# Delta rule of a two-block network: convolutions, gate curves and the gates' softplus chain planned as lanes of their own

## The chip, the cores and the metric

One Trainium2 chip, one NeuronCore. The time is the device time of one execution of the whole program in microseconds (us), median of three executions. Beside it one execution was taken by the hardware profiler; all rows below are from that one.

## What is computed

Two residual blocks on 512 tokens of width 1024, in fp32, one after the other. The change touches one stage, the gated delta rule that opens the second block. Cut to what matters:

```python
qkv = silu(_causal_dwconv(concat([qa, ka, va]), conv_w))        # 4 taps, 3 x 8 heads of 128 channels
q = l2norm(q) * 128**-0.5;  k = l2norm(k)
beta = sigmoid(beta)
g = -exp(a_log) * softplus(alpha + dt_bias);  G = cumsum(g)      # within chunks of 64 tokens
decay = where(incl, exp(G_i - G_j), 0)
L = where(strict, beta * (k k^T) * decay, 0)
sol = triangular_solve(I + L, [beta*v, beta*exp(G)*k])           # per head and chunk
# scan over 8 chunks: U = u - w S; o = q_dec S + p_intra U; S = S*e + k_dec^T U
oa = rmsnorm(o) * silu(za)
y  = sigmoid(ga) * (oa @ w_a_out) + sigmoid(gb) * (ob @ w_b_out) # ob: band attention, the next stage
x  = x + y @ w_o
```

## The kernel before

**An order made on the host.** `order()` writes one list of steps for the whole program before anything runs. Each of the five engine programs (`tensor_program`, `scalar_program`, `vector_program`, `gpsimd_program`, `sync_program`) walks through this list and issues its own part of every step, so every engine executes in the list's order and waits on semaphores where a result is needed. Within a stage the list is made by `weave()`: several generators ("lanes"), each at a time of its own on a planner's clock, and the lane with the earliest time goes next. The costs by which that clock moves are the table `ROUGH` (engine T, V, A or G, fixed us, us for each block). A step with parts on two engines is one entry of the list: its DVE part and its ACT part take their places in both engines' queues at once.

**The stage.** Weights come in units of 1 MB (256 columns) into two buffers. Each unit is split into a high and a low fp32r part (ScalarE L2002, GpSimd L2800), and a tile of 128 x 512 outputs is 24 matmuls of 512 columns (L1750) into one PSUM bank. The product stream (`products`) has two banks (`sbank`), the other lanes six (`fbank`). The stream makes for each head h the tiles q, k and v (`project`), with the band gate's tiles `gb` after chosen ones, then `za`, `ga` and at the end `wa2`.

**A tile's way.** `dq1` multiplies the bank by the row of norms (L2268) into one of two padded buffers, which frees the bank, and starts the convolution with the first tap (L2572). `dq2` is the other three taps in one step (L2578), `dq3` is SiLU on ScalarE (L2128). The three steps stand in the product stream itself, behind the tile's matmuls. `project(h)` begins once head h-2 is prepared to the end, since the convolved q, k, v have two places each. `GATES_AFTER` says where `gb` tiles (`band_gate`, step `gb`: L2268, then Sigmoid L2209) go in.

**The gates.** `gates1` (L2268, Sigmoid L2106), `gates2` (softplus, with Exp L2109 and Ln L2112) and `gates3` (cumulative sum, Exp L2115) follow one another in the lane `gates()` with no yield between them. Their results, turned and split, are what every head's decay needs (`rct`, `rlo`).

**A head.** `prepare(h)` starts once `cooked` holds h (q, k and v all through SiLU), head h-2 is inverted and the pair before the last is scanned. It turns k (`p8`), forms k k^T (`p11`), sums squares (`p2`, L2139), and `p4` makes the decay: two DVE operations, Exp on ScalarE (L2143), five small DVE operations and a multiplication. `p12` multiplies k k^T by it (L2629). Then `invert(h)` (two lanes, even and odd heads) begins with `i1` (L2648, L2650), turns the matrix on TensorE (L1781, copy back L2163) and goes through five levels of two products each (L1786; DVE L2655, L2659). `i7u` and `i7w` apply the inverse; each has its product and its copy (L2169) in one step. `scan(g)` runs over the eight chunks of a pair of heads (L1904, L1913, L1923, L1926; DVE L2673, L2685), `gate(g)` norms and multiplies by silu(za) (step `za`: L2268, Silu L2179), `ga` is L2268 and Sigmoid L2183, `ya` multiplies the projected output by it (L2706), `ysum` and `yop` do so for the other branch and split the sum for `w_o`.

## Time and profile before

| | us |
|---|---|
| median of 3 executions | 2621.57 (2620.88 to 2621.96) |
| profiled execution, its own time | 2616.85 |
| its span, first to last instruction | 2615.6 |
| the changed stage in it | about 1196 to 1747 |
| TensorE busy, share of the span | 2525.3 (97%) |

The profiled execution was 4.7 us (0.18%) shorter than the median. A matmul's busy time overlaps the next one's: a busy TensorE is one that waits for nothing, not one at its peak. The granted clock has two levels, 2.4 GHz (1.00) and 1.2 GHz.

### The profile page before, as it was taken

Reading aid. Unit: us, or ns where it says so; the run is one execution under the profiler, and the core shown is the slowest. Engines: PE = TensorE matmul, PEld = TensorE weight load, DVE = VectorE, ACT = ScalarE, POOL = GpSimd, SP = SyncE. Lnnn points to the kernel's source line nnn. Section 1 sums busy time; section 2 is a strip of 40 time slices with the busy share of each in tenths; the row PEclk is TensorE's granted clock in tenths of the full one; section 3 lists DMA queues with packets and bytes.
Section 4 is the critical chain, followed back from the end, with each engine's and each line's share of the span. In section 5 each row is a group of like instructions: output and inputs, shape, how many; then the busy total and the mean of one; then the engine's idle time right before and its main releaser. Section 6 shows DMA issues by size and latency. Waiting matters only on the chain.

```text
span 2615.6 us, 32476 instructions
## 1 busy us (share of the span) xinstructions
PE 2525.3 (97%) x12760; PEld 2076.0 (79%) x12760; DVE 1054.0 (40%) x2281; ACT 951.9 (36%) x1448; POOL 1171.1 (45%) x1565
## 2 busy tenths in 40 slices
PE   7999999999999999999999999999999999999997
PEld 5777888888777888887888888877767887888886
DVE  6964111125963111125657664413444423310112
ACT  4553322234553222234434333315453434321221
POOL 5115665653115655654323221453224664565653
PEclk9999999999999999999999999999999999999999
DMA  4442223224532223223111110132212322222222
GB/s 160 126 113 81 97 83 103 97 89 141 135 95 81 97 94 108 92 80 119 65 49 49 49 49 33 65 113 81 90 57 97 113 97 81 97 87 99 99 91 76
DMA packets 41367, 237.27 MB, mean 91 GB/s; under 512 B 4736, under 2 KB 5888, under 8 KB 18560
## 3 DMA queue, kind: packets, MB, share of 16 engines
q1 hardware_dynamic: 38912, 218.43, 24.0%
q0 software_dynamic: 2304, 16.78, 3.2%
q8 instruction: 101, 1.65, 0.3%
q14 instruction: 50, 0.41, 0.1%
HBM read 214.22 MB, written 4.19 MB: 84 GB/s over the span
## 4 chain that ended last, share of the span: by engine, by line
PE 84%; DVE 9%; ACT 3%; POOL 2%; issue 1%; DMA 1%; SPq 0%; DVEq 0%; ACTq 0%; POOLq 0%
PE PB L1750 68%; PE PB L1752 3%; PE PB L1786 3%; POOL WL L2800 2%; DVE cc L2409 1%; PE PB L1770 1%; ACT WH L2002 1%; PE PB L1938 1%; PE PB L1762 1%; PE PB L1957 1%; PE PB L1945 1%; PE PB L1822 1%; PE PB L1781 1%; PE PB L1969 1%; PE PB L1985 1%
## 5 line engine op out<-in xcount | busy, mean ns | idle before, releaser
L2800 POOL TENSOR_TENSOR WL<-WR,WH 128x256 fp32r<-128x256 f32 (+1 forms) x1444 | 1043.5, 759 | 876.6 <-ACT WH L2002 876.6
L1750 PE MATMUL PB<-HH,WH 128*128 128x512 f32 x1992 | 805.2, 404 | 14.6 <-ACT HH L2017 9.8
L1750 PE MATMUL PB<-HL,WH 128*128 128x512 f32 x1992 | 782.6, 393 | 2.0 <-DVE HL L2303 2.0
L1750 PE MATMUL PB<-HH,WL 128*128 128x512 f32 x1992 | 519.4, 396 | 1.1 <-POOL WL L2800 1.1
L1750 PEld LDWEIGHTS PB<-HH,WH 128*128 128x128 f32 x1992 | 377.6, 190 | 105.5 <-issue 15.6
L2002 ACT ACTIVATE WH<-WR 128x2048 fp32r<-128x2048 f32 (+1 forms) x209 | 371.5, 1778 | 227.7 <-PE PB L1750 221.4
L1750 PEld LDWEIGHTS PB<-HL,WH 128*128 128x128 f32 x1992 | 377.6, 190 | 80.1 <-issue 4.6
L1750 PEld LDWEIGHTS PB<-HH,WL 128*128 128x128 f32 x1992 | 366.4, 189 | 74.6 <-issue 3.4
L1750 PE MATMUL PB<-BL,WH 128*128 128x512 f32 x848 | 334.1, 394 | 0.8 <-DVE BL L2312 0.8
L1750 PE MATMUL PB<-BH,WH 128*128 128x512 f32 x784 | 311.5, 397 | 2.7 <-ACT BH L2031 2.7
L1750 PE MATMUL PB<-BH,WL 128*128 128x512 f32 x784 | 196.4, 395 | 4.5 <-POOL WL L2800 4.5
L2318 DVE TENSOR_TENSOR X<-X,PB 128x512 f32<-128x512 f32 x80 | 54.9, 687 | 354.6 <-PE PB L1750 354.6
L1750 PEld LDWEIGHTS PB<-BL,WH 128*128 128x128 f32 x848 | 160.8, 190 | 37.2 <-DVE BL L2312 1.5
L1750 PEld LDWEIGHTS PB<-BH,WH 128*128 128x128 f32 x784 | 148.8, 190 | 37.7 <-ACT BH L2031 4.4
L1750 PEld LDWEIGHTS PB<-BH,WL 128*128 128x128 f32 x784 | 147.9, 189 | 38.6 <-POOL WL L2800 5.7
L2813 POOL TENSOR_TENSOR BL<-ff1c,BH 128x512 fp32r<-128x512 f32 x44 | 56.9, 1294 | 169.7 <-ACT BH L2031 169.7
L2031 ACT ACTIVATE BH<-ff1c 128x512 fp32r<-128x512 f32 x44 | 27.8, 632 | 233.3 <-DVE ff1c L2501 233.3
L2268 DVE TENSOR_TENSOR ff1b<-PB,RSTD 128x512 f32<-128x512 f32 x44 | 30.4, 691 | 196.5 <-PE PB L1750 196.5
L2268 DVE TENSOR_TENSOR ff1a<-PB,RSTD 128x512 f32<-128x512 f32 x44 | 30.4, 692 | 174.6 <-PE PB L1750 167.7
L2806 POOL DMA_DIRECT2D WL<-WR x16 | 14.1, 884 | 190.1 <-ACT WL L2005 190.1
L2409 DVE SCALAR_TENSOR_TENSOR cc<-cp,VECS,cc 128x512 f32<-128x512 f32 x120 | 93.3, 830 | 0.0
L2017 ACT ACTIVATE HH<-X,VECS 128x512 fp32r<-128x512 f32 x48 | 33.2, 718 | 122.5 <-DVE X L2318 122.5
(348 smaller groups left out, 2933.0 us busy)
## 6 DMA issues: line engine op xcount, KB each, us to landing
WR<-in_w_gu SPq DMA_DIRECT2D x66, 1024.0 KB, 4.8
WR<-in_w_dn SPq DMA_DIRECT2D x48, 704.0 KB, 4.0
WR<-in_w_in SPq DMA_DIRECT2D x22, 1024.0 KB, 4.9
WL<-WR POOLq DMA_DIRECT2D x16, 1024.0 KB, 7.5
WR<-in_qkv SPq DMA_DIRECT2D x12, 1024.0 KB, 4.9
WR<-in_w_out SPq DMA_DIRECT2D x8, 1024.0 KB, 4.8
WR<-in_qk SPq DMA_DIRECT2D x8, 1024.0 KB, 4.9
WR<-in_gb SPq DMA_DIRECT2D x4, 1024.0 KB, 4.9
```

What stands on the lines that cost most here:

```text
L1750: ins = pe.matmul(out[:, 0:n], wt[:, k * cols + j * P:k * cols + (j + 1) * P], x[:, k, 0:n], start=first, stop=last)
L1752: ins = pe.matmul(out[:, 0:cols], x[:, k, j * P:(j + 1) * P], wt[:, k * cols:(k + 1) * cols], start=first, stop=last)
L1762: ins = pe.matmul(out[:, j0 + b:j0 + b + 1], blk(src, b), ones[:, 0:1], start=(j0 == 0 and b == 0), stop=(b == nb - 1), skip_group_check=True)
L1786: ins = pe.matmul(blk(PB[t.b], i), blk(left, i), blk(right, i), start=True, stop=True)
L2002: a.activation(m.WH[u % 2][:, 0:n], m.WR[u % 2][:, 0:n], ACT.Copy).then_inc(sems["whi"], 1)
L2017: a.activation(m.HH[:, c, :], m.X[:, c, :], ACT.Copy, scale=w["gain"]).then_inc(sems["hh"], 1)
L2031: a.activation(high[:, w["c"], :], w["src"], ACT.Copy).then_inc(sems["bh"], 1)
L2268: v.tensor_tensor(dst, PB[t.b][:, 0:bank_cols], m.RSTD[:], ALU.mult).then_inc(sems[name], 1)
L2318: v.tensor_tensor(m.X[:, c, :], m.X[:, c, :], PB[w["tile"].b][:], ALU.add).then_inc(sems["res"], 1)
L2409: v.scalar_tensor_tensor(m.cc[j][:], m.cp[j][:, k:k + S], vec(f"dw_w{l}", 2 * k + j), m.cc[j][:], ALU.mult, ALU.add).then_inc(sems["tap"], 1)
L2800: ins = g.tensor_tensor(m.WL[u % 2][:, part], m.WR[u % 2][:, part], f32(m.WH[u % 2][:, part]), ALU.subtract)
L2813: g.tensor_tensor(m.BL[:, w["c"], :], w["src"], f32(high[:, w["c"], :]), ALU.subtract).then_inc(sems["blg"], 1)
```

## The change

- The convolution leaves the product stream. `dq1` is now only the multiplication that frees the bank. Each of the four taps is a step `dq2` with a key of its own, in a new lane `convolutions()`, with SiLU (`dq3`) a step behind them. A tap waits for `read[j]` of head h-2 (that the old q, k or v has been read), each of the three alone. The stream no longer waits for head h-2; it waits for a free padded buffer.
- `prepare(h)` starts when the keys are through SiLU (`curved[1]`), and its second half waits for q and v. A new `due()` holds it in the plan until the planner's clock says that the signal is there.
- `gates2` becomes `soft1`, `soft2`, `soft3` with a yield behind each.
- `p4` is split into `p4`, `p4n`, `p4d`; the curves of `za`, `ga` and `gb` become steps `zact`, `gact`, `gbact`, the last two in lanes of their own; `i7u` and `i7w` do their products together and then the copies `i8u`, `i8w`.
- Sigmoid of `ga` and `gb` becomes Tanh of half the argument; `ya` and `ysum` multiply by (t + 1) in the same instruction and `yop` takes the factor 0.5.
- `ROUGH` gets new costs for these steps.

```diff
-    "gates1": [("V", 0.8, 0), ("A", 1.9, 0)], "gates2": [("V", 1.5, 0), ("A", 2.0, 0), ("V", 0.6, 0), ("A", 1.9, 0), ("V", 3.0, 0)],
-    "gates3": [("V", 2.0, 0), ("A", 3.0, 0)], "gates4": [("T", 0.5, 0), ("A", 0.5, 0)], "gates5": [("A", 1.4, 0), ("V", 0.8, 0)],
-    "rs2": [("V", 3.5, 0)], "nt": [("V", 0.9, 0)], "dq1": [("V", 1.3, 0)], "dq2": [("V", 2.5, 0)], "dq3": [("A", 1.3, 0)],
+    "gates1": [("V", 0.7, 0), ("A", 1.9, 0)], "soft1": [("V", 1.2, 0), ("A", 2.1, 0)], "soft2": [("V", 0.5, 0), ("A", 1.9, 0)], "soft3": [("V", 2.6, 0)],
+    "gates3": [("V", 2.4, 0), ("A", 2.6, 0)], "gates4": [("T", 0.5, 0), ("A", 0.5, 0)], "gates5": [("A", 1.4, 0), ("V", 0.8, 0)],
+    "rs2": [("V", 3.5, 0)], "nt": [("V", 0.9, 0)], "dq1": [("V", 0.72, 0)], "dq2": [("V", 0.78, 0)], "dq3": [("A", 1.3, 0)],
...
-"p4": [("V", 1.5, 0), ("A", 0.7, 0), ("V", 1.2, 0)], "p6": [("V", 3.5, 0)], "p5": [("T", 0.5, 0)],
+"p4": [("V", 1.4, 0), ("A", 2.0, 0)], "p4n": [("V", 0.85, 0)], "p4d": [("V", 0.75, 0)], "p6": [("V", 2.4, 0)], "p5": [("T", 0.5, 0)],
...
@@ project
-                pd = pads.take()
-                step("dq1", h, j, tile=t, pad=pd.i, after=pd.after, c_after=cfree["qkv"[j] + str(i)])
+                while all(x.held for x in pads.rooms):
+                    yield
+                pad_of[h, j] = pd = pads.take()
+                step("dq1", h, j, tile=t, pad=pd.i, after=pd.after)
                 room.free(at("dq1", h, j))
                 yield
-                step("dq2", h, j, pad=pd.i)
-                pd.free(at("dq2", h, j))
-                yield
-                step("dq3", h, j)
...
+        def convolutions():
+
+            for h in range(8):
+                for j in range(3):
+                    while (h, j) not in pad_of:
+                        yield
+                    yield from until((read[j], h - 2))
+                    pd = pad_of[h, j]
+                    for k in (3, 2, 1, 0):
+                        step("dq2", h, j, k, pad=pd.i, tok=at("dq1", h, j), c_after=cfree["qkv"[j] + str(h % 2)])
+                        if k == 0:
+                            pd.free(at("dq2", h, j, 0))
+                        yield
+                    step("dq3", h, j)
+                    curved[j].add(h)
+                    yield
+
+        def curves_b():
+            for c in range(DC):
+                while c not in gb_in:
+                    yield
+                step("gbact", c, tok=at("gb1", c))
+                gb_out.add(c)
+                yield
...
@@ prepare
             ready.add(h)
             yield
+            yield from until((curved[0], h), (curved[2], h))
+            yield from due(at("dq3", h, 2))
...
+        def due(*signals):
+
+            while clock.known(list(signals)) > max(clock.lane, clock.free["T"]):
+                yield
...
@@ products
             for h in range(8):
-                yield from until((prepared, h - 2))
                 yield from project(h)
...
@@ preparations
-                yield from until((cooked, h), (inverted, h - 2), (scanned, h // 2 - 2))
-                yield
-                yield
+                yield from until((curved[1], h), (inverted, h - 2), (scanned, h // 2 - 2))
+                yield from due(at("dq3", h, 1))
...
-            a.activation(m.SGA[:, c, :], m.SGA[:, c, :], ACT.Sigmoid).then_inc(sems["ga"], 1)
+            a.activation(m.SGA[:, c, :], m.SGA[:, c, :], ACT.Tanh, scale=0.5).then_inc(sems["ga"], 1)
...
-            v.tensor_tensor(m.SGA[:, c, :], PB[w["tile"].b][:], m.SGA[:, c, :], ALU.mult).then_inc(sems["ya"], 1)
+            v.scalar_tensor_tensor(m.SGA[:, c, :], m.SGA[:, c, :], 1.0, PB[w["tile"].b][:], ALU.add, ALU.mult).then_inc(sems["ya"], 1)
```

## Rows read from the trace of the kernel before

**Rows 1.** The page's first line.

```profile
span 2615.6 us, 32476 instructions
```

**Rows 2.** Windows: from:to, length, busy us and instructions by engine, PEclk, DMA share, GB/s.

```profile
1196.00:1747.00 551.00, 528.75 (x3121) 453.86 (x3120) 316.35 (x723) 209.18 (x365) 173.39 (x233) 0.99 0.17 59
...
1220.00:1240.00 20.00, 19.55 (x89) 16.17 (x90) 16.26 (x25) 10.50 (x19) 8.97 (x11) 0.91 0.15 53
1240.00:1260.00 20.00, 15.98 (x84) 13.55 (x83) 13.11 (x31) 11.54 (x19) 10.27 (x14) 0.91 0.16 53
```

**Rows 3.** Waits of TensorE in 1196 to 1747: waiter, releaser, us, times, longest.

```profile
PE PB L1781 <- DVE ZZ L2650: 7.0, 6, 4.0
PE PB L1786 <- ACT TT L2163: 6.1, 3, 2.1
PE PB L1750 <- DVE pad L2268: 4.9, 2, 3.4
```

**Rows 4.** Timeline of TensorE: start, us, line, operands, count, [idle before it].

```profile
1205.79 0.50 PE L1750 MATMUL PB<-HH,WH 128*128 128x512 f32 x1 [1.41 <-DVE pad L2268]
...
1214.13 0.39 PE L1750 MATMUL PB<-HH,WH 128*128 128x512 f32 x1
1214.36 0.39 PE L1750 MATMUL PB<-HL,WH 128*128 128x512 f32 x1
...
1220.45 0.50 PE L1750 MATMUL PB<-HH,WH 128*128 128x512 f32 x1 [3.44 <-DVE pad L2268]
...
1222.16 0.63 PE L1750 MATMUL PB<-HH,WH 128*128 128x512 f32 x1
1222.58 0.63 PE L1750 MATMUL PB<-HL,WH 128*128 128x512 f32 x1
...
1245.87 1.09 PE L1781 MATMUL PB<-CON,ZZ 128*128 128x128 f32 x4 [4.02 <-DVE ZZ L2650]
...
1347.41 1.54 PE L1786 MATMUL PB<-TT,UM 128*128 128x128 f32 x8 [2.07 <-ACT TT L2163]
...
1521.14 1.26 PE L1786 MATMUL PB<-TT,UM 128*128 128x128 f32 x8 [1.99 <-ACT TT L2163]
```

**Rows 5.** Timeline of DVE: the multiplication that ends the first long wait.

```profile
1219.71 0.69 DVE L2268 TENSOR_TENSOR pad<-PB,RSTD 128x512 f32<-128x512 f32 x1
```

**Rows 6.** Timeline of DVE and ACT before the wait that ends at 1347.41.

```profile
1342.73 3.38 DVE L2578 SCALAR_TENSOR_TENSOR ck<-pad,VECS,ck 128x512 f32<-128x512 f32 x3
...
1346.15 0.63 ACT L2128 ACTIVATE ck<-ck 128x512 f32<-128x512 f32 x1 [5.09 <-DVE ck L2578]
1346.69 0.58 ACT L2163 ACTIVATE TT<-PB 128x512 f32<-128x512 f32 x1
```

**Rows 7.** Timeline of ACT: the first head's exponential, and two later heads'.

```profile
1238.95 1.28 ACT L2209 ACT_TABLE_LOAD   x1
...
1240.90 1.28 ACT L2143 ACT_TABLE_LOAD   x1
1242.19 0.63 ACT L2143 ACTIVATE DT<-DT 128x512 f32<-128x512 f32 x1
...
1473.72 0.63 ACT L2143 ACTIVATE DT<-DT 128x512 f32<-128x512 f32 x1 [2.56 <-DVE DT L2591]
...
1539.47 0.63 ACT L2143 ACTIVATE DT<-DT 128x512 f32<-128x512 f32 x1 [0.36 <-DVE DT L2591]
```

**Rows 8.** Groups by line in 1474 to 1539, TensorE: count, busy us, mean ns.

```profile
L1750 PE MATMUL PB<-HH,WH 128*128 128x512 f32 x38 | 16.8, 441 | 0.0
```

**Rows 9.** Groups by line in 1195 to 1750: count, busy us, mean ns, idle before.

```profile
L2578 DVE SCALAR_TENSOR_TENSOR cq<-pad,VECS,cq 128x512 f32<-128x512 f32 x24 | 18.0, 751 | 0.8
...
L2209 ACT ACT_TABLE_LOAD x5 | 6.4, 1283 | 0.1
...
L2694 DVE SCALAR_TENSOR_TENSOR O<-O,VECS,PB 128x512 f32<-128x512 f32 x8 | 5.9, 743 | 3.5 <-PE PB L1770 3.5
...
L2706 DVE TENSOR_TENSOR SGA<-PB,SGA 128x512 f32<-128x512 f32 x8 | 5.5, 692 | 40.4 <-PE PB L1750 40.4
```

More of the change, by code:

```diff
@@ L1030, in gates @@
             bank0.free(at("ab"))
-            step("gates2", after=f)
+            step("soft1", after=f)
+            yield
+            step("soft2", after=f)
+            yield
+            step("soft3", after=f)
+            yield
             step("gates3", after=f)
@@ L1094, in project, with curves_a @@
                         yield from band_gate()
-            cooked.add(h)
+        pad_of = {}
+        def convolutions():
[16 more added lines that the diff above has]
+                while c not in gb_in:
+                    yield
+                step("gbact", c, tok=at("gb1", c))
+                gb_out.add(c)
+                yield
+        def curves_a():
+            for c in range(DC):
+                while c not in ga_in:
+                    yield
+                step("gact", c, tok=at("ga1", c))
+                ga_out.add(c)
+                yield
         kn_done = [[], []]
@@ L1112, in prepare @@
             step("p4", h, tile=t, after=dt_after[0] + hf)
+            step("p4n", h, tile=t)
+            yield
+            step("p4d", h, tile=t)
             room.free(at("pdn", h))
@@ L1124, in prepare @@
             cfree[f"v{i}"] = [t4.done]
+            read[2].add(h)
             step("p1", h, q=qq.i, after=qq.after)
@@ L1185, in invert @@
             yield from until((prepared, h))
-            yield from fbank.left(1)
-            room = fbank.take()
-            t = Tile(room, room.after)
-            pe("i7u", h, tile=t, after=st_after)
-            room.free(at("iut", h))
-            yield from fbank.left(1)
-            room = fbank.take()
-            t = Tile(room, room.after)
-            ifree[f"Z{i}"] = half_after[i] = [pe("i7w", h, tile=t, after=st_after)]
-            room.free(at("iwt", h))
+            yield from fbank.left(2)
+            room, t = row("i7u", h)
+            room2, t2 = row("i7w", h)
+            ifree[f"Z{i}"] = half_after[i] = [t2.done]
+            step("i8u", h, tile=t, after=st_after)
+            room.free(at("iut", h))
+            step("i8w", h, tile=t2, after=st_after)
+            room2.free(at("iwt", h))
             yield
@@ L1249, in gate @@
                     yield
+                step("zact", h, tok=at("za1", h))
+                yield
                 yield from fbank.left(1)
@@ L1274, in gate_tiles @@
                 drain(itg)
-        cooked, ready, prepared, inverted, scanned, gated, gated_heads = (set() for _ in range(7))
+        ready, prepared, inverted, scanned, gated, gated_heads = (set() for _ in range(6))
+        curved, read = [set() for _ in "qkv"], [set() for _ in "qkv"]
         def until(*conditions):
@@ L1306, in products @@
                     room, t = x
+                    while c not in ga_out:
+                        yield
                     step("ya", c, tile=t)
@@ L1355, in operands @@
                 yield
-        weave(clock, products(), 0.0, lane(gates(), preparations()), inversions(0), inversions(1), scans(), gatings(), last_gating(), operands())
+        weave(clock, products(), 0.0, lane(gates(), preparations()), inversions(0), inversions(1), scans(), gatings(), last_gating(), operands(),
+              convolutions(), curves_b(), curves_a())
     def band_attention(xs):
@@ L2106, in scalar_program @@
             a.activation(m.R[32:64, :], m.UM[0][32:64, :], ACT.Sigmoid).then_inc(sems["beta"], 1)
-        elif kind == "gates2":
+        elif kind == "soft1":
             ae.wait_ge(*at("dtb"))
@@ L2163, in scalar_program @@
             a.activation(m.TT[key[0] % 2][:], PB[w["tile"].b][:], ACT.Copy).then_inc(sems["it"], 1)
-        elif kind in ("i7u", "i7w"):
+        elif kind in ("i8u", "i8w"):
             h, = key
@@ L2528, in vector_program @@
             times_rstd(m.UM[0][:], w["tile"], "ab")
-        elif kind == "gates2":
+        elif kind == "soft1":
             ve.wait_ge(*at("ab"))
@@ L2567, in vector_program @@
             ve.all(w["after"])
[L2568 removed]
             times_rstd(m.pad[w["pad"]][:, 3:3 + S], w["tile"], "dq1")
[L2570 to L2572 removed]
         elif kind == "dq2":
[L2574 to L2581 removed]
+            h, j, k = key
+            c, pad = m.cqkv[h % 2][j], m.pad[w["pad"]]
+            tap = vec("conv2", 24 * k + 8 * j + h)
+            if k == 3:
+                ve.wait_ge(*at("dq1", h, j))
+                ve.all(w["c_after"])
+                v.tensor_scalar(c[:], pad[:, 3:3 + S], tap, None, ALU.mult).then_inc(sems["dq2"], 1)
+            else:
+                ve.wait_ge(*at("dq2", h, j, k + 1))
+                v.scalar_tensor_tensor(c[:], pad[:, k:k + S], tap, c[:], ALU.mult, ALU.add).then_inc(sems["dq2"], 1)
         elif kind == "p4":
```

64 lines of the change are left out of this document (30 added, 34 removed), and 12 rows, old and new, of tables (KINDS, ROUGH).

## The prediction

> **What bounds the kernel now.** I read the page's head first [rows 1], then windows over the changed stage [rows 2], TensorE's list of waits in it [rows 3], its timeline at the longest waits [rows 4], and for each the timelines of the engine named [rows 5 to 7]. In the stage's 551.0 us TensorE is busy for 528.75: it waits 22.25 us, and DVE (316 us), ScalarE (209 us) and GpSimd (173 us) are far from full. So the stage is bound by TensorE's own work, and neither fewer DVE nor fewer ScalarE microseconds are worth anything as such. What an order of steps can give back is the 22.25 us and what follows from it. The clock is the second part: four stretches of 20 us (from 1220, 1240, 1340 and 1520; the first two in [rows 2]) show a granted clock of 0.91 instead of 1.00, each one with a wait of about 2 to 4 us before or in it. Behind the wait that ends at 1220.45 the engine falls to the 1.2 GHz level: matmuls that start 0.23 us apart at 1214 start 0.42 us apart at 1222 [rows 4]. A mean of 0.91 over 20 us is 3.6 us at half speed, which costs at most 1.8 us; I count seven matmuls 0.2 us too long in the first stretch, 1.4 us. I take 1.5 for each of four, 6.0 us in all.
>
> So the ceiling of the change is about 22.25 + 6 = 28 us, 1.1% of the kernel. The rest of this text sorts that sum by cause.
>
> **The gates' chain in one piece.** TensorE waits 3.44 us until 1220.45 for a product bank, and the DVE multiplication that would free it starts only at 1219.71 [rows 4, 5]. A tile is 24 matmuls 0.225 us apart, 5.4 us; the one in question began at 1205.79 [rows 4] and was done by about 1211.4. Its `dq1` stands in DVE's queue behind gates2 and gates3. With a yield behind each of soft1, soft2 and soft3, a `dq1` of 0.69 us can stand between them. Then the wait goes, and the half-speed stretch with it: 3.4 + 1.5 = 4.9. The other 1.5 us of L2268's 4.9 [rows 3] come before, when the norms themselves are made, and the change leaves them. What is late next: the gates' results, by the DVE work that is let in front of them, one or two `dq1` and a few taps, 0.7 to 4 us. Behind them stands the first head's decay.
>
> **The first head.** TensorE waits 4.02 us for the first inversion's matrix [rows 4]. Two things work on it. Before, head 0 waits until q, k and v are all through SiLU, and head 1's q convolution is in DVE's queue ahead of its decay (four taps, of which three take 2.3 us in the mean, [rows 9]); now it starts with k alone. I rebuild DVE's work from 1205 with the durations of the trace: dq1 and taps of q 3.6, ab and soft1 1.9, dq1 of k 0.7, soft2 and soft3 3.3, gates3 2.3, dq1 of v 0.7, taps of k 2.9, splitting the gates 3.1: about 1224. Add the decay (1.4, the exponential with its load 1.9, four more operations 2.8) and some 3 us for what else is let in: the first matrix is there at 1233 to 1237, not at 1245.8. Dense work for TensorE up to there is q, k, v, q of head 1 and two `gb` tiles at 5.4 us each, which reaches to about 1236. The second is ScalarE's side: 1.28 us for a table load for the band gate's Sigmoid at 1238.95, 0.63 us for the curve, and 1.28 us for a load back at 1240.90 lie directly ahead of that exponential [rows 7]. Either is enough for most of the 4.02. I take 4.0 + 1.5 = 5.5. If the dense cover is short by the time the gates' chain gets longer, up to 4 us of it stay.
>
> The Trainium skill bears on the second part (ScalarE: Activation LUTs, *Table sets: the hidden batching unit*): tanh is in the set that has exp as its anchor, so Tanh beside Exp needs one load and not two. By it one of the two 1.28 us loads at 1238.95 and 1240.90 goes, and the others of L2209 that stand behind an exponential. The same page prices a switch at about 2.66 us with its drain, and by that the chain of head 0 would gain 2.66 us instead of 1.28; this case's trace shows the activation 0.01 us behind the 1.28 us load, so the trace disagrees with the drain. None of this enters the sum, which has the 4.02 us once whichever part removes it.
>
> **The convolution in one piece.** Three waits of TensorE, 6.1 us, are for L2163, the copy of a turned matrix [rows 3]. The one that ends at 1347.41 shows why [rows 6]: DVE works on three taps without a break, from 1342.73 for 3.38 us, SiLU on them waits in ScalarE's queue for 5.09 us and runs at 1346.15, and the copy, whose input TensorE made at 1344, comes behind SiLU at 1346.69. The waiting instruction blocks its queue. In the new list SiLU is a step that comes when the plan has the last tap done, and the copy, planned earlier, stands ahead of it. All three have this form (1521.14 is another). The waits go, and with them two of the four half-speed stretches, those of 1340 and 1520: 6.1 + 3.0 = 9.1. What can remain: a tap can now stand between an inversion's own DVE steps, 0.75 us in the mean [rows 9] and up to 1.13 where GpSimd is busy [rows 6]; and with wrong costs SiLU can still be planned too early. I keep 2 us of it: 7.1.
>
> **The decay's cost in the plan.** Five more waits for L2650, together 7.0 - 4.0 = 3.0 us [rows 3], come at the start of a head's inversion: the plan had 0.7 us for an exponential that takes 1.28 + 0.63 = 1.9 [rows 7], so TensorE's turn came about 1.2 us early. The new cost is 2.0. I take 2.0 of the 3.0.
>
> **What costs nothing.** The new instructions are as many as the old ones. `ya` and `ysum` change from a two-input multiplication to one with a scalar, of which the trace has 692 ns (L2706) and 743 ns (L2694) for the same size [rows 9]: 0 to 0.05 us each, 24 of them with `yop`. DVE idles 40.4 us before the eight L2706 [rows 9], so this hides behind the projection's matmuls; without cover it is at most 1.2 us. Tanh is not in the trace; the nearest row is the exponential of the same size, 0.63 us [rows 7], and a table load of 1.28 us more or less. A set for tanh of its own would be loaded where Sigmoid's is now, five times for L2209 [rows 9] and twice for L2183, so no worse than before. Every DMA keeps its order and number; SP's queue only follows the units. The joint products i7u and i7w ask for three free banks of six instead of two, which can hold a lane back, not TensorE.
>
> **The sum.** 4.9 + 5.5 + 7.1 + 2.0 = 19.5 us gone. Against it I set new waits. The old order lost 22.25 us in 551; some 10 of it are taken by these terms' twins in any order: DVE slowed from 0.75 to 1.13 us by GpSimd, copies behind a 1.9 us split on ScalarE, none of it in the plan. A different order meets these at other places. I take 5 us (between 0 and 12). Net: 14.5. Against the profiled execution, 2616.85 - 14.5 = 2602.4; the median of the runs shown lies 4.7 us higher, so 2607.
>
> **The rivals.**
> 1. *All of it comes* and few new waits appear: 19.5 us or more, up to 28: 2602 down to 2594. For it speaks that heads start some 10 us earlier, so that the plan always has something ready. Against: nothing in the plan knows of contention.
> 2. *New waits take the place of the old.* Finer steps give as many chances to be wrong as before; the four causes go and others of 10 to 17 us in total come. Net 8 us to a loss of 4: 2614 to 2626. For it: 2 us of TensorE's waits are enough to lose 1.5 more by the clock.
> 3. *The filler is used up too early* (slower). The stream no longer waits for head h-2, so it can run ahead by two padded buffers and two banks, four tiles. Between the exponentials of head 5 (1473.72) and head 6 (1539.47) [rows 7] TensorE has the last q, k, v tiles and scans as dense and small work: 38 high matmuls are 4.8 tiles [rows 8]. Four of them moved ahead leave 4 x 5.4 = 21.6 us of that gap to be filled by two inversions and a scan alone. If these can't, it costs 21.6 and two half-speed stretches, 3.0, less the 14.5: 2607 + 24.6 = 2632. It decides from 14.5 us lost there. Against it: the small work in the gap fills about 35 us by itself, and the gap shrinks as the chains get TensorE sooner; the work moved ahead is not lost.
> 4. *The table loads decide*: silu, exp and tanh alternate more often, each 1.28 us on ScalarE. ScalarE is busy 209 of 551 us, so ten more loads show only where TensorE waits for a copy. This is part of rival 2.
>
> **How the numbers follow.** The likeliest case, 9 to 19 us gained, 2602 to 2613: 0.50. Rival 1, below 2602: 0.18. Rivals 2 and 4, 2613 to 2626: 0.21. Rival 3, above 2626: 0.11. The predicted time is 2607. For 8 in 10 I go from 2596, where only the ceiling's last two microseconds are left out, to 2622, into rival 2. About 0.2% (5.2 us) is what a measurement of this kernel can tell from no change. Faster than 2616.3: the first two cases and a third of rival 2, 0.75. Within 0.2%: the rest of rival 2, 0.14. Slower: rival 3 whole, 0.11.
>
> **What would show it.** In the profile after: no wait on L2268 of 3 us near 1215 to 1220; the first L1781 on ZZ before 1240 with no 4 us before it; no wait of about 2 us on L2163's copy; in ScalarE's timeline SiLU of a convolution starting within 1 us of getting to the queue's head; granted clock 1.00 in nearly all 20 us stretches; in total 8 to 13 us of TensorE waiting in the stage. The prediction is wrong if TensorE's waits add up to 20 us at other places, if the stage's busy time itself grows (more changes between dense and small matmuls), or if waits gather between head 5 and head 6.

## The result, and the profile after

The changed kernel takes 2586.97 us (median of 4 runs, 2585.19 to 2594.96) where the kernel before, run beside it, takes 2621.23 us (median of 4, 2615.5 to 2621.96). The medians are 34.3 us apart (1.3%); the ratio over all the runs is 0.9886, 95% interval 0.9871 to 0.9900, so 1.0 to 1.3% faster. The forecast was 2607 with a range of 2596 to 2622. The sign was right; the size was outside the range, on the side of rival 1 and beyond it.

The page of the profile after, its first line and the busy time of the engines (device time of this execution 2587.04 us):

```profile
span 2585.7 us, 32474 instructions
...
PE 2513.4 (97%) x12760; PEld 2069.5 (80%) x12760; DVE 1051.3 (41%) x2281; ACT 943.9 (37%) x1440; POOL 1181.1 (46%) x1565
```

The windows over the changed stage, with the same 3,121 to 3,123 matmuls as [rows 2], and the four stretches that had a granted clock of 0.91 before:

```profile
1195.50:1719.50 524.00, 518.85 (x3123) 449.99 (x3122) 314.72 (x723) 201.22 (x357) 182.07 (x233) 1.00 0.18 62
...
1220.00:1240.00 20.00, 20.00 (x98) 16.72 (x97) 15.60 (x26) 13.17 (x23) 9.65 (x13) 1.00 0.31 106
1240.00:1260.00 20.00, 19.06 (x110) 16.20 (x110) 16.80 (x38) 8.01 (x15) 8.85 (x12) 1.00 0.28 96
1340.00:1360.00 20.00, 20.00 (x128) 17.62 (x128) 13.58 (x27) 9.57 (x20) 7.00 (x8) 1.00 0.04 6
1520.00:1540.00 20.00, 20.00 (x132) 17.65 (x131) 15.45 (x39) 8.38 (x18) 6.17 (x8) 1.00 0.15 53
```

TensorE is idle for 5.2 us of 524, where it was 22.25 of 551, and the clock is 1.00 throughout; the prediction had 8 to 13 us of waiting. The list of TensorE's waits in this stage (L1799 is the dense matmul, L1750 before; L1830 the turns, L1781 before; L2318 was L2268, L2714 was L2659):

```profile
PE PB L1799 <- DVE pad L2318: 1.4, 1, 1.4
PE PB L1799 <- POOL WL L2855: 1.3, 1, 1.3
PE PB L1830 <- DVE ZZ L2714: 1.1, 2, 0.9
PE PB L1819 <- DVE STAT L2392: 0.7, 1, 0.7
PE PB L1962 <- DVE UU L2728: 0.6, 1, 0.6
```

All that was named in [rows 3] is gone but for 1.4 of L2268's 4.9. The lines of 1.4, 1.3 and 0.7 stand in the list of before too. New are only 1.1 + 0.6 = 1.7 us.

The gates' chain, DVE's timeline: DVE now waits for TensorE's tiles (last brackets), where TensorE waited for DVE in [rows 4, 5].

```profile
1210.98 0.69 DVE L2318 TENSOR_TENSOR pad<-PB,RSTD 128x512 f32<-128x512 f32 x1 [2.01 <-PE PB L1799]
1211.59 0.74 DVE L2631 SCALAR_TENSOR_TENSOR cq<-pad,VECS,cq 128x512 f32<-128x512 f32 x1
...
1216.49 0.69 DVE L2318 TENSOR_TENSOR pad<-PB,RSTD 128x512 f32<-128x512 f32 x1 [3.82 <-PE PB L1799]
```

The first head, TensorE's timeline: the turn of the first inversion runs at 1247.06 with no wait.

```profile
1245.49 0.60 PE L1830 MATMUL PB<-CON,cv 128*128 128x128 f32 x4
...
1247.06 0.60 PE L1830 MATMUL PB<-CON,ZZ 128*128 128x128 f32 x4
```

But its input is not early. DVE's row that ends it starts at 1243.24:

```profile
1243.24 0.69 DVE L2705 TENSOR_TENSOR ZZ<-CON,ZZ 128x512 f32<-128x512 f32 x1
```

The forecast had the matrix at 1233 to 1237; it was there at 1243.9, 39.5 us after the stage's first padded product, where it took 40.7 us before. TensorE came to the place of this turn 36.8 us after that product before, and 42.6 us after it now, since the plan has a dense tile, a turn and two small groups ahead of it (1240.05 to 1247.06). So the wait went for the larger part by the turn's later place, and for 1.3 us of the 4.0 by an earlier matrix.

ScalarE and the convolutions. These groups (count, busy us, mean ns, then ScalarE's idle time before them and what ended it) are L2128 of the kernel before:

```profile
L2128 ACT ACTIVATE cv<-cv 128x512 f32<-128x512 f32 x8 | 5.1, 632 | 24.2 <-DVE cv L2578 24.2
...
L2128 ACT ACTIVATE cq<-cq 128x512 f32<-128x512 f32 x8 | 5.1, 632 | 23.5 <-DVE cq L2578 23.5
...
L2128 ACT ACTIVATE ck<-ck 128x512 f32<-128x512 f32 x8 | 5.0, 631 | 30.2 <-DVE ck L2578 30.2
```

and the same after, with the table loads left there:

```profile
L2178 ACT ACT_TABLE_LOAD x8 | 10.3, 1283 | 0.1
L2193 ACT ACT_TABLE_LOAD x8 | 10.3, 1283 | 0.1
L2178 ACT ACTIVATE cq<-cq 128x512 f32<-128x512 f32 x8 | 5.0, 629 | 0.1
L2178 ACT ACTIVATE cv<-cv 128x512 f32<-128x512 f32 x8 | 5.0, 628 | 3.7 <-DVE cv L2631 3.7
L2178 ACT ACTIVATE ck<-ck 128x512 f32<-128x512 f32 x8 | 5.0, 627 | 5.3 <-DVE ck L2631 5.2
```

SiLU held ScalarE's queue for 24.2 + 23.5 + 30.2 = 78 us while it waited for taps, and now for 9. That is the mechanism of [rows 6], and the change removes nearly all of it. The loads of the band gates (L2209, five, and L2183, two) are gone.

### The profile page after: what moved, and what is told of

It reads as the page before. It is cut to its first block, busy times and chain, and to the rows that moved or that the text cites. A ratio compares the mean times of both kernels' runs of the same rounds, so it can differ in the third digit from the quotient of the medians.

```text
span 2585.7 us, 32474 instructions
## 1 busy us (share of the span) xinstructions
PE 2513.4 (97%) x12760; PEld 2069.5 (80%) x12760; DVE 1051.3 (41%) x2281; ACT 943.9 (37%) x1440; POOL 1181.1 (46%) x1565
## 3 DMA queue, kind: packets, MB, share of 16 engines
q1 hardware_dynamic: 38912, 218.43, 24.2%
## 4 chain that ended last, share of the span: by engine, by line
PE 88%; DVE 7%; POOL 2%; ACT 1%; issue 1%; DMA 0%; SPq 0%; DVEq 0%; ACTq 0%; POOLq 0%
PE PB L1799 71%; PE PB L1835 4%; PE PB L1801 3%; DVE cc L2459 2%; POOL WL L2855 2%; PE PB L1830 1%; PE PB L1811 1%; PE PB L1819 1%; PE PB L2006 1%; PE PB L1987 1%; PE PB L1994 1%; PE PB L1871 1%; PE PB L2034 1%; PE PB L2018 1%; PE PB L1975 1%
## 5 line engine op out<-in xcount | busy, mean ns | idle before, releaser
L1799 PE MATMUL PB<-HH,WH 128*128 128x512 f32 x1992 | 801.5, 402 | 11.3 <-ACT HH L2066 9.9
L1799 PE MATMUL PB<-HL,WH 128*128 128x512 f32 x1992 | 779.5, 391 | 1.9 <-DVE HL L2353 1.9
L1799 PE MATMUL PB<-HH,WL 128*128 128x512 f32 x1992 | 520.6, 396 | 1.1 <-POOL WL L2855 1.1
L1799 PEld LDWEIGHTS PB<-HH,WH 128*128 128x128 f32 x1992 | 375.9, 189 | 101.9 <-issue 16.0
L1799 PEld LDWEIGHTS PB<-HL,WH 128*128 128x128 f32 x1992 | 375.9, 189 | 80.5 <-issue 4.8
L1799 PEld LDWEIGHTS PB<-HH,WL 128*128 128x128 f32 x1992 | 365.0, 188 | 74.7 <-issue 4.4
L1799 PE MATMUL PB<-BL,WH 128*128 128x512 f32 x848 | 332.8, 392 | 0.8 <-DVE BL L2362 0.8
L1799 PE MATMUL PB<-BH,WH 128*128 128x512 f32 x784 | 309.7, 395 | 2.7 <-ACT BH L2080 2.7
L1799 PE MATMUL PB<-BH,WL 128*128 128x512 f32 x784 | 196.7, 395 | 4.5 <-POOL WL L2855 4.5
L1799 PEld LDWEIGHTS PB<-BL,WH 128*128 128x128 f32 x848 | 159.7, 188 | 36.9 <-DVE BL L2362 1.5
L1799 PEld LDWEIGHTS PB<-BH,WL 128*128 128x128 f32 x784 | 148.1, 189 | 38.7 <-POOL WL L2855 5.7
L1799 PEld LDWEIGHTS PB<-BH,WH 128*128 128x128 f32 x784 | 148.0, 189 | 38.1 <-ACT BH L2080 5.1
L2318 DVE TENSOR_TENSOR ff1b<-PB,RSTD 128x512 f32<-128x512 f32 x44 | 30.4, 691 | 196.5 <-PE PB L1799 196.5
L2318 DVE TENSOR_TENSOR ff1a<-PB,RSTD 128x512 f32<-128x512 f32 x44 | 30.4, 692 | 175.2 <-PE PB L1799 167.7
```

The lines of the kernel that those rows point to most:

```text
L1799: ins = pe.matmul(out[:, 0:n], wt[:, k * cols + j * P:k * cols + (j + 1) * P], x[:, k, 0:n], start=first, stop=last)
L2318: v.tensor_tensor(dst, PB[t.b][:, 0:bank_cols], m.RSTD[:], ALU.mult).then_inc(sems[name], 1)
```

## Where the 30 us of the profiled executions went

I cut the span at two events that every version has: the start of the first padded product (1205.0 before, 1204.5 after) and the start of the last `ya` (1744.0, 1716.3). TensorE issues 3,069 or 3,070 matmuls between them in every version. The windows of exactly these stretches, of the kernel before:

```profile
1205.00:1744.00 539.00, 518.07 (x3069) 445.76 (x3070) 310.80 (x705) 205.40 (x363) 164.39 (x221) 0.99 0.16 55
```

and after:

```profile
1204.50:1716.30 511.80, 508.06 (x3070) 441.75 (x3071) 309.19 (x706) 197.46 (x354) 173.07 (x221) 1.00 0.17 58
```

The stage is 27.2 us shorter. Idle TensorE: 20.9 to 3.7, 17.2 us. The clock: four stretches at 0.91 are 4 x 20 x 0.09 = 7.2 us, and after there is none. The other 2.8 us are busy time that neither explains. Outside the stage the profiled executions differ by another 2.7 us: 0.5 ahead of it, 6.4 in the stretch behind it (275.7 to 269.3), and 4.2 back in the rest. The stretch behind it ends at the last `SGA<-SGA,X` (2019.7 and 1985.6). From the last `ya` to the end of the program both kernels, and all versions below, give TensorE the same instructions in the same order, and the stretch takes 267.8 to 276.9 us in them. In the kernels before (first line) and after TensorE is idle there for the same 16.8 us, and the clock differs:

```profile
1744.00:2019.70 275.70, 258.91 (x1581) 203.74 (x1581) 110.80 (x329) 122.91 (x282) 97.36 (x144) 0.96 0.25 88
1716.30:1985.60 269.30, 252.46 (x1580) 199.01 (x1579) 111.46 (x328) 122.77 (x282) 98.52 (x144) 0.99 0.25 86
```

The kernels with the old steps have 268.6 to 275.7 us there and those with the new ones 267.8 to 276.9, so I don't count the 6.4 as the change's.

All kernels of this study by the same cut. Clock is the sum of 20 us times (1 - granted clock) over the stretches of 20 us in the stage; the medians stand beside a kernel before of 2619.9 to 2621.4 us in each group of runs.

```
                                    stage  busy   idle  clock  median us  ratio, 95%
before                              539.0  518.1  20.9   7.2   2621.23
after                               511.8  508.1   3.7   0.0   2586.97    0.9871 to 0.9900
e1_before_newcosts                  554.1  523.0  31.1  15.8   2631.03    1.0026 to 1.0051
e2_sigmoid                          511.8  508.1   3.7   0.0   2591.70    0.9864 to 0.9918
e4_all_three                        510.7  507.3   3.4   0.0   2586.58    0.9844 to 0.9900
e3_throttle                         520.9  512.5   8.4   5.2   2603.25    0.9920 to 0.9956
e5_gates_one                        519.9  510.8   9.1   1.8   2595.16    0.9883 to 0.9919
e6_taps_one                         522.0  509.3  12.7   0.0   2596.40    0.9893 to 0.9944
e8_old_costs                        519.5  512.0   7.5   3.4   2595.57    0.9886 to 0.9936
e13_three_undone                    536.7  520.0  16.7  15.6   2610.68    0.9953 to 0.9981
e10_stall                           520.9  510.5  10.4   3.4   2602.31    0.9915 to 0.9962
f1_line                             513.9  508.5   5.4   0.0   2590.87    0.9855 to 0.9901
new steps, costs: p1_costs_up  +6%  543.3  523.4  19.9  13.8   2622.32    0.9998 to 1.0020
                  p3_up3       +3%  524.3  512.7  11.6   3.4   2605.47    0.9913 to 0.9959
                  p4_down3     -3%  516.9  511.3   5.6   3.4   2593.52    0.9884 to 0.9926
                  p2_costs_down -6% 510.4  506.8   3.6   0.0   2592.15    0.9868 to 0.9922
old steps, costs: q1_old_up    +6%  546.5  520.4  26.1  10.6   2625.65    1.0014 to 1.0037
                  q3_old_up3   +3%  550.1  522.6  27.5  14.0   2625.41    1.0002 to 1.0025
                  q4_old_down3 -3%  533.9  517.2  16.7   5.4   2610.04    0.9960 to 0.9979
                  q2_old_down  -6%  548.1  525.6  22.5  15.4   2622.68    0.9999 to 1.0025
```

Busy time less clock is 507 to 512 us in all but one (504 in e13). (The idle 3.7 and 20.9 us are less than the 5.2 and 22.25 above: a wait of 0.7 us and the first half of the one of 1.4 us lie ahead of the cut.) So the stage is some 509 us of TensorE's work, plus its idle time, plus the clock. The clock's part tends to grow with the idle part, none at 3.7 us and 7 to 16 where some 20 us or more are idle, but loosely: none at 12.7 us in e6. It is one profiled execution of each kernel, while one kernel's executions differ by up to 10 us (2585.19 to 2594.96 for after); a difference of a few us between two rows needs the medians beside it.

## The experiments

**The costs alone on the old steps** (e1_before_newcosts; the new planner costs of the head's preparation, the gates and the taps in the kernel before):

```
-  "p4": [("V", 1.5, 0), ("A", 0.7, 0), ("V", 1.2, 0)], "p6": [("V", 3.5, 0)]
+  "p4": [("V", 1.4, 0), ("A", 2.0, 0), ("V", 1.6, 0)], "p6": [("V", 2.4, 0)]
...
-  "dq1": [("V", 1.3, 0)], "dq2": [("V", 2.5, 0)]
+  "dq1": [("V", 1.2, 0)], "dq2": [("V", 2.34, 0)]
```

> The kernel before with the planner's new costs alone (gates, p4, p6, dq1, dq2), no step split. Theory A (the finer steps make the gain): the five short waits for the first turn of a head go and the early 4 us wait shrinks, but the waits of about 2 us on the copy L2163 and the 3.4 us wait for the product bank stay: 3 to 8 us faster than before, 2613 to 2618. Theory B (the right costs make the gain): 15 us or more faster, under 2606. Theory C (each order is a draw): anywhere within 10 us of before.

2631.03 us, 10 us slower than before. Theories A and B missed; C, a draw within 10 us of before, is missed by 0.4 us. The waits that the prediction had tied to the costs did go (L2650 has one of 1.8 us left of 7.0), but others grew or came:

```profile
PE PB L1786 <- ACT TT L2163: 8.1, 5, 3.6
PE PB L1750 <- DVE pad L2268: 4.9, 2, 3.4
PE PB L1786 <- DVE YY L2655: 4.5, 2, 3.5
```

Better costs by themselves gave a worse order here.

**One part undone at a time.** The stream of projections limited to two heads ahead again (e3_throttle):

```
             for h in range(8):
+                yield from until((prepared, h - 2))
                 yield from project(h)
```

> The new kernel with one line put back: the product stream waits until head h-2 is prepared to the end. Theory A: the running ahead isn't what helps; within 4 us of the new kernel, 2583 to 2591. Rival: dense tiles ready early are the cover that the old order lacked; waits come back, 2595 or more.

The four taps and SiLU in one piece (e6_taps_one):

```
                             pd.free(at("dq2", h, j, 0))
-                        yield
                     step("dq3", h, j)
```

> The new kernel with the four taps and SiLU of a convolution planned as one piece again (no yield between them), still in a lane of their own. Theory A: the waits of about 2 us on the copy of a turned matrix come back, three or more of them with their half-speed stretches, +6 to +12 us against the new kernel: 2593 to 2599. Theory B: nothing, since the costs are right: 2585 to 2590.

The gates' chain in one piece (e5_gates_one; its third gate tiles also wait for the last value head, a line that f1_line tries alone):

```
             step("soft1", after=f)
-            yield
             step("soft2", after=f)
-            yield
             step("soft3", after=f)
-            yield
```

> The new kernel with soft1, soft2, soft3 and gates3 in one piece (and the gate tiles waiting for the last v besides). Theory A: the wait of 3 to 4 us for a product bank near 1217 comes back and a half-speed stretch behind it: +5 us, 2592. If the new order had room for it anyway: no change within 2 us.

The old costs of a head and of the convolution in the new steps, the gates' costs staying new (e8_old_costs):

```
-  "p4": [("V", 1.4, 0), ("A", 2.0, 0)], "p4n": [("V", 0.85, 0)], "p4d": [("V", 0.75, 0)], "p6": [("V", 2.4, 0)]
+  "p4": [("V", 1.5, 0), ("A", 0.7, 0)], "p4n": [("V", 0.6, 0)], "p4d": [("V", 0.6, 0)], "p6": [("V", 3.5, 0)]
...
```

> The new kernel with the old planner costs for a head (exponential of the decay 0.7 us instead of 2.0, p6 3.5 instead of 2.4, the convolution's 3.15 in all). The first experiment showed the new costs alone in the old steps to be slower by 10 us. Theory A (finer steps make the gain, costs add little): 2587 to 2594. Theory B (both are needed: a plan of fine steps is only as good as its costs): waits for the first turn of each head come back, eight of 0.5 to 2 us with half-speed stretches, 2597 or more.

The stages are 9.1, 10.2, 8.1 and 7.7 us longer than after's, the medians 16.3, 9.4, 8.2 and 8.6. e3 met its rival (2595 or more), e6 the time of its theory A by other waits than that theory's, e5 lost more than its theory A, and e8 fell between its two. For none of them is the loss mainly the return of the wait that the prediction had tied to the part. e3 has 2.9 us at `YY` and 1.7 at `SMALL`. Of the gates' 3.44 us wait e5 has 1.24 back:

```profile
1217.86 0.50 PE L1796 MATMUL PB<-HH,WH 128*128 128x512 f32 x1 [1.24 <-DVE pad L2315]
```

e8's list has no wait for the first matrix of a head. e6 brings SiLU's hold on ScalarE back, here its three groups,

```profile
L2177 ACT ACTIVATE cv<-cv 128x512 f32<-128x512 f32 x8 | 5.1, 632 | 21.8 <-DVE cv L2630 21.8
L2177 ACT ACTIVATE cq<-cq 128x512 f32<-128x512 f32 x8 | 5.1, 632 | 19.5 <-DVE cq L2630 19.5
L2177 ACT ACTIVATE ck<-ck 128x512 f32<-128x512 f32 x8 | 5.1, 632 | 23.3 <-DVE ck L2630 23.3
```

65 us of idle ScalarE against 9, but none of TensorE's 2 us waits for the turned copy: its waits are 4.2 us at `YY` and 2.3 at `ZZ`. A blocked ScalarE costs nothing where the order has nothing of TensorE's behind it.

**The three structural parts undone together** (e13_three_undone, the edits of e3, e5 and e6 in one):

> The new kernel with three parts undone together: the stream waits for head h-2, the taps are one piece, the gates' chain is one piece. Alone they cost the stage 9.1, 10.2 and 8.1 us. If they add up: 511.8 + 27.4 = 539.2 us, the old kernel's time. If each only moves the order to another draw: about as one alone, 518 to 526.

2610.68 us, 23.7 more than after; the sum of the single parts was 27.4 us in the stage, and here it is 24.9 (536.7 us). That is near the adding up of 539.2 and outside the 518 to 526 of another draw; it is one order. The old first wait is back to within 0.01 us, at 1219.42, where [rows 4] had 3.44 at 1220.45:

```profile
1219.42 0.79 PE L1796 MATMUL PB<-HH,WH 128*128 128x512 f32 x1 [3.45 <-DVE pad L2315]
```

e5, with the gates alone in one piece, has 1.24 us of it. The other 2.2 us are the taps' and SiLU's. The projections can't be the cause here: their limit holds nothing back for heads 0 and 1, and e3 has every instruction of the three engines TensorE, DVE and ScalarE in after's order until 1247. ScalarE's timeline shows the way, first e13, then e5 (L2152 is the gates' sigmoid, with which their chain begins):

```profile
1207.62 0.63 ACT L2175 ACTIVATE cq<-cq 128x512 f32<-128x512 f32 x1 [3.64 <-DVE cq L2628]
...
1209.57 0.63 ACT L2152 ACTIVATE R<-UM 32x512 f32<-32x512 f32 x1
...
1207.34 0.63 ACT L2152 ACTIVATE R<-UM 32x512 f32<-32x512 f32 x1 [1.37 <-DVE UM L2315]
```

With the taps in one piece SiLU of the first q stands at the head of ScalarE's queue for 3.64 us, and the gates' sigmoid behind it, with a load of 1.28 us between them that e5 has done before its sigmoid's input is there. Counted from the first padded product the chain begins 2.9 us later, and the multiplication that frees the bank comes 2.2 us later (14.66 us against 12.42; before: 14.66). So the split taps alone take two thirds of this wait away, by the mechanism of [rows 6], and the cut chain alone takes all of it: e6, with the taps in one piece, waits for a padded tile only the 1.4 us that every version has. The two parts meet in one wait; the prediction gave it to the gates.

**The parts that give nothing.** Sigmoid in place of tanh (e2_sigmoid), TensorE's order being the same instruction for instruction:

```
-            a.activation(m.SGA[:, c, :], m.SGA[:, c, :], ACT.Tanh, scale=0.5).then_inc(sems["ga"], 1)
+            a.activation(m.SGA[:, c, :], m.SGA[:, c, :], ACT.Sigmoid).then_inc(sems["ga"], 1)
...
```

> The new kernel with Sigmoid for both gates again, every step in the same place, TensorE's order identical. Rows of the two traces: seven table loads for the gates' curves are gone in the new one. If they lay beside other work, as the prediction has it but for one: +0 to +2 us, 2587 to 2589. If ScalarE's queue is as full as the copies it serves: each load delays a copy that TensorE waits for, +5 us or more, 2592.

And a head prepared only when q, k and v are all there (e4_all_three):

```
-                yield from until((curved[1], h), (inverted, h - 2), (scanned, h // 2 - 2))
+                yield from until((curved[0], h), (curved[1], h), (curved[2], h), (inverted, h - 2), ...)
-                yield from due(at("dq3", h, 1))
+                yield from due(at("dq3", h, 2))
```

> The new kernel with a head's preparation waiting for q, k and v together. Theory A: heads start a tile later, but the stage is bound by TensorE's work: within 4 us of the new kernel, 2584 to 2591. Rival: the keys' start is what keeps the inversions ahead of the scans: +8 us, 2595 or more.

Their stages are 511.8 and 510.7 us, against 511.8. Sigmoid brings ScalarE 34 loads in five groups where there are 18 in three,

```profile
L2178 ACT ACT_TABLE_LOAD x11 | 14.1, 1283 | 0.2
L2193 ACT ACT_TABLE_LOAD x8 | 10.3, 1283 | 0.1
L2259 ACT ACT_TABLE_LOAD x6 | 7.7, 1283 | 0.1
L2229 ACT ACT_TABLE_LOAD x5 | 6.4, 1283 | 0.1
L2233 ACT ACT_TABLE_LOAD x4 | 5.1, 1283 | 0.1
```

16 x 1.28 = 20.5 us more on ScalarE and nothing on TensorE. Its median, 2591.70, lies 4.7 above after's; the intervals overlap, and the profile has the difference behind the stage (275.4 against 269.3), where nothing was changed for TensorE.

**The price of a wait** (e10_stall): 17 small VectorE operations with their waits ahead of the fifth `ya`, whose results nobody uses.

```
             ve.wait_ge(*at("ga", c))
+            if c == 4:
+                for _ in range(17):
+                    dv.link(v.tensor_scalar(m.DT[:], m.RSTD[:], 1.0, None, ALU.mult))
+                    dv.wait()
```

> The new kernel with one wait made on purpose, where nothing else runs: 17 DVE copies of about 0.5 us ahead of the fifth product of the output projection, whose bank TensorE needs two tiles later. It should wait some 3 to 4 us there, once. If a wait costs its own length only: new kernel plus that length, 2590 to 2591. If the clock's fall behind it costs 1.5 us more, as the prediction took it: 2592, and a granted clock near 0.91 in that stretch of 20 us.

TensorE's timeline at the made wait:

```profile
1714.16 0.79 PE L1799 MATMUL PB<-OH,WH 128*128 128x512 f32 x1 [6.73 <-DVE SGA L2765]
```

and the two windows around it:

```profile
1700.00:1720.00 20.00, 13.27 (x49) 10.30 (x49) 12.21 (x19) 1.91 (x1) 12.47 (x16) 0.83 0.45 155
1720.00:1740.00 20.00, 20.00 (x96) 16.71 (x95) 2.76 (x4) 3.40 (x2) 2.85 (x8) 1.00 0.31 108
```

A made wait of 6.73 us lengthens the stage by 9.1: 6.7 idle and 2.4 of busy time, by a stretch at 0.83 (20 x 0.17 = 3.4). The wait is longer than the 3 to 4 us that were expected, and 2602.31 is above both forecasts. The whole kernel's median is 15.3 us longer, and in the profile 7.6 lie in the stretch behind (276.9 against 269.3), with 16.6 us idle there and a clock of 0.95. 276.9 is the longest that this stretch shows, and all four executions took 2601.67 us or more. Whether a part of these 7.6 us belongs to the wait is not shown; 9.1 is the least that it cost.

**The order as a draw.** First VectorE's costs in the plan 6% up or down with the new steps, and 6% up with the old ones (p1_costs_up, p2_costs_down, q1_old_up). Ten costs of VectorE in the old plan, twelve in the new:

```
-  "dq1": [("V", 0.72, 0)], "dq2": [("V", 0.78, 0)]
+  "dq1": [("V", 0.763, 0)], "dq2": [("V", 0.827, 0)]
...
```

> The new kernel with the planner's DVE costs of the stage 6% higher (and the gate tiles waiting for the last v), nothing else: another draw of an order from the new steps. The stage, from the first padded multiplication to the last product with the gate, took 539.0 us before and 511.8 in the new kernel. Theory A (the finer steps make orders good in general): 510 to 517 us. Theory C (the new order is a lucky draw): 520 us or more, as the experiments that undid one part gave 519.5 to 522.

> The same with the costs 6% lower. Theory A: 510 to 517 us for the stage. Theory C: 520 us or more.

> The old kernel with its DVE costs 6% higher: another draw from the old steps. The old steps with the old costs gave 539.0 us for the stage, with the new costs 554.1. Theory A: 532 to 555. Theory C: the spread of the old steps reaches the new kernel's, under 525.

p1 takes the whole gain away: 2622.32 us and a stage of 543.3, as theory C has it; p2 (510.4) and q1 (546.5) came as theory A has them. The three largest lines of its list of waits are none of those in [rows 3]:

```profile
PE PB L1835 <- DVE YY L2710: 4.7, 4, 2.8
PE PB L1962 <- DVE UU L2728: 4.1, 1, 4.1
PE PB L1811 <- ACT SQ L2084: 4.1, 1, 4.1
```

ScalarE's timeline of p1 ahead of the last of these, which ends at 1569.03:

```profile
1562.55 1.28 ACT L2193 ACT_TABLE_LOAD   x1
1565.63 0.63 ACT L2193 ACTIVATE DT<-DT 128x512 f32<-128x512 f32 x1 [1.81 <-DVE DT L2640]
1566.28 1.28 ACT L2229 ACT_TABLE_LOAD   x1
1567.58 0.63 ACT L2229 ACTIVATE z<-z 128x512 f32<-128x512 f32 x1
1568.11 0.26 ACT L2224 ACTIVATE O<-PB 128x128 f32<-128x128 f32 x1
1568.27 0.62 ACT L2084 ACTIVATE SQ<-O 128x512 f32<-128x512 f32 x1
```

The square that TensorE needs stands behind an exponential that waits 1.81 us for VectorE, between two loads. It is the pattern of [rows 6] again, an instruction at a queue's head that waits for another engine, with the steps as fine as the change makes them; SiLU's own hold is only 7 us in p1. Fine steps remove one such place; whether others arise is up to the order. (p3_up3 has three waits for the turned copy again, 3.1 us in all, the longest 2.0.)

Then the line that p1 and p2 carried besides (f1_line), and costs 3% up and down, and the old steps 3% up, 3% and 6% down.

```
-            yield from until((prepared, 6))
+            yield from until((prepared, 6), (curved[2], 7))
             yield from gate_tiles(2)
```

> The new kernel with nothing but one more wait in the plan: the third gate tiles also wait until the last value head's curve is placed, a line that the runs with costs 6% up and down carried too. If that line is harmless (it comes after nearly all of the heads), 2583 to 2593. If it, and not the costs 6% up, took the gain away there, 2610 to 2625.

> The new kernel with VectorE's costs in the plan 3% up (and the line of f1_line). Theory S, the new steps carry the gain and 6% up was a rare bad order: 2585 to 2600, with under 10 us of idle TensorE in the stage. Theory D, the gain is mostly the order that the plan happens to fall into: anything from 2585 to 2622, and one of this and p4_down3 at 2608 or more.

> The new kernel with VectorE's costs in the plan 3% down (and the line of f1_line). Theory S, the new steps carry the gain: 2585 to 2600. Theory D, the gain is mostly the order that the plan happens to fall into: anything from 2585 to 2622, and one of this and p3_up3 at 2608 or more.

> The kernel before with VectorE's costs in its plan 3% up. Theory S: 2612 to 2632, as the three orders of the old steps measured so far (2621 to 2631), with 18 us or more of idle TensorE in the stage. Theory D: the old steps too fall into good orders now and then, and one of this, q4_old_down3 and q2_old_down is at 2608 or less.

> The kernel before with VectorE's costs in its plan 3% down. Theory S: 2612 to 2632. Theory D: one of this, q3_old_up3 and q2_old_down is at 2608 or less.

> The kernel before with VectorE's costs in its plan 6% down. Theory S: 2612 to 2632. Theory D: one of this, q3_old_up3 and q4_old_down3 is at 2608 or less. By theory S the six orders of the old steps and the seven of the new ones hardly overlap, and their means differ by 20 us or more; by theory D the means differ by less than 12 us.

The line is harmless: its interval overlaps after's. The five orders of the new steps (costs as they are, 3% and 6% up and down) have a mean of 2600.1 us and lie between 2587.0 and 2622.3; the five of the old steps 2621.0, between 2610.0 and 2625.7. The means differ by 20.9 us, with a standard error of 7 from the two spreads; with so few orders that makes a 95% interval of about 4 to 38 us, which leaves out zero and says little of the size. Without the two kernels as they were given, the four nudged orders of each differ by 17.6 us with an error of 8, which alone doesn't leave out zero. Mean idle time in the stage is 22.7 us with the old steps and 8.9 with the new.

Theory S's difference of means came. Its ranges did not: p1 (2622.32), p3 (2605.47, 11.6 us idle) and q4 (2610.04, 16.7 us idle) lie outside them. Theory D's marks did not come: no order of the old steps is at 2608 or less, neither p3 nor p4 is at 2608 or more, and the means differ by more than 12. But the new steps do reach from 2587 to 2622, as it has them. Neither was right alone.

## Why the prediction was wrong

- **What bounds the kernel, and the ceiling.** Right for the stage. Its gain is TensorE's waits, 17.2 us, the clock, 7.2, and 2.8 of busy time that the sum didn't have; together 27.2, under the ceiling of 28. The medians differ by 34.3, more than the ceiling; the rest lies outside the stage, where one order shows 267.8 to 276.9 us.
- **The clock.** 1.5 us were taken for each of the four stretches, 6.0; by 0.09 x 20 = 1.8 each, all came, 7.2 (this sum can be too high: e10 has 3.4 by it and 2.4 in busy time). That the clock falls at a wait is shown by e10_stall with a wait that I made: 2.4 us beyond 6.7. That each wait costs its share is not so: e6 is idle for 12.7 us and loses none.
- **The gates' chain, 4.9.** The wait went, and the cut chain is enough for it, as predicted (e6 has none of it). But 2.2 of the 3.44 us would have gone without that cut: they came from SiLU of the first q, which stood ahead of the gates' sigmoid on ScalarE (e13 against e5). The prediction looked at DVE's queue alone.
- **The convolution, 7.1.** The named waits went. SiLU's 78 us of hold fell to 9, and e6 brings 65 back, so the queue mechanism is shown, and at the gates it has a price, 2.2 us with their chain in one piece. What isn't shown is that the 6.1 us of [rows 3] are its price: with the hold back and another order, those waits aren't there. And not all of them have quite the form of [rows 6]: ahead of the copy of the one that ends at 1509.89, a weight split of 1.89 us stands between SiLU (1506.92) and the copy (1509.26).
- **The first head, 5.5.** The wait went, in the main for a reason that was not mine. The matrix came at 1243.9 and not at 1233 to 1237: my sum had the durations of DVE's operations and left out its own waits between them, 2.0, 3.8 and 2.4 us up to the end of the gates' splitting at 1231.2, where I had about 1224. And e4_all_three shows that the start with k alone is worth nothing in the stage (-1.1 us). The load in front of the exponential was worth nothing either (e2_sigmoid).
- **The decay's cost, 2.0.** On the old steps the new costs made 10 us of loss (e1); on the new steps the old ones cost 8.6 us (e8 against after), by other waits than those named. In both cases it is one order against another, within what nudged costs do, so the 2.0 us are neither shown nor refuted.
- **The step that failed** is the sum's last: "A different order meets these at other places. I take 5 us (between 0 and 12)", with the 3 us kept of the convolution's and the costs' waits. No row gave the 5 us; it was a guess. This order had 1.7 us of new waits and kept nothing: 17.2 instead of 13.5 - 5 = 8.5. Of the 8.7 between them, 3.3 are the new waits, 3.0 what was kept, and some 2.4 small old waits that the sum didn't name (the largest 1.3 us in two at `UU`). They are the larger part of the 12.7 us by which the stage beat the forecast (27.2 against 14.5); 1.2 is the clock, 2.8 busy time. Another 2.7 lie outside the stage, where TensorE's order is the same (luck, as far as is known), and 4.7 is the offset from the profiled execution to the median, which was added, while the median after stands at its own profiled time (2586.97, 2587.04). 12.7 + 2.7 + 4.7 = 20.1, the miss.
- **Was 5 us a bad figure?** As a mean, hardly: the forecast left 20.9 - 8.5 = 12.4 us idle, the five orders of the new steps have 3.6 to 19.9 with a mean of 8.9, and their mean time, 2600.1, lies inside the range. The error was to take an order's luck as one residual term with a range of its own, 0 to 12 us, when the clock and the old order's luck move with it. The new steps alone spread over 35 us with cost changes that nobody would call a change. Of its five orders the range of 2596 to 2622 holds one, 2605.5: it was too narrow on the fast side, and its slow end is just what 6% in the costs gives.
- **The rivals.** Rival 1 is the nearest: in the stage 27.2 of its 28 us came, and the median lies 7 us below its end of 2594. Rival 2 is what p1 did, 2622. Rival 3 did not come: between heads 5 and 6 no wait is longer than 0.6 us, and with the projections held back again the stage is 9.1 us longer, where the rival has it shorter, though one order each way can't size it. Rival 4 fell with e2: 16 more loads, no time.
- What stays open: which of the parts carries how much of the 21 us. Single parts undone lengthen the stage by 8 to 10 us each, less than the new steps' own spread, and only several orders of each would tell. One order of either kernel says little of the steps: after is the fastest of its five.

## What to carry over

A host-side plan that fixes in-order queues is a draw: before a change of steps is credited or blamed, nudge the plan's costs by a few per cent both ways in both kernels and compare the means; here about 21 us (give or take 7) came with the steps and about 13 with the order. Split the stage into work, idle time and clock of the bounding engine at events that all versions share: it shows at once which part moved. And look for instructions that wait at the head of a queue (ScalarE idle before SiLU, 78 us), on every engine of the chain behind a wait and not only on the one that the profile names, but price them only by what the bounding engine waits for.

## What the runs showed of the hardware that was not expected

- Tanh loaded no table, neither after the exponential (1266.99, tanh at 1277.42 without a load) nor after SiLU (1227.24, tanh at 1231.97): 16 of them, no load, and all seven of the sigmoids' in the kernel before gone. The Trainium skill (ScalarE: Activation LUTs, *Table sets: the hidden batching unit*) leads one to expect the first of these.
- The clock's part is not one sum for each wait. Idle time of 12.7 us in small pieces (e6, none over 2.1) cost no clock at all; 16.7 us cost 5.4 in one order and 15.6 in another.
- The same TensorE instructions in the same order behind the stage took 267.8 (p4_down3) to 276.9 us (e10_stall) in the versions' profiled executions, with 17.0 and 16.6 us idle and a mean clock of 1.00 and 0.95.
